# An inference step of a hybrid encoder on one core: the mLSTM's denominators, four weight blocks of the output projection, and four evictions change their place or engine

## The chip, the cores and the metric

The program runs on one NeuronCore of a Trainium2 chip. A core has five engines that run side by side, each its own instructions in a fixed order: TensorE (in profiles PE; its weight loads are PEld), VectorE (DVE), ScalarE (ACT), GpSimd (POOL) and SyncE (SP), which here only starts transfers. They meet at semaphores: an instruction waits until a counter that other engines raise has reached a number. Data lie in SBUF (128 partitions); TensorE writes its products into PSUM, which has eight banks here. The metric is the device time of one launch in microseconds (us); lower is better.

## The reference, cut to what matters

One step of a trunk of two layers over 1024 prompt tokens and 32 sample tokens, model width 1024, all in fp32. Layer 0 mixes with a gated recurrence (RG-LRU) and sliding-window attention side by side, layer 1 with the mLSTM matrix memory. Behind each mixer stands a SwiGLU and a gated per-layer term.

```python
# layer 0: attention of a chunk's queries over its own and the two earlier chunks, with sinks
s = einsum('...qkgd,...skd->...kgqs', q, k) * B_HEAD_DIM ** -0.5 + bias      # bias = -slope * distance
p = softmax(concatenate([s, sink], axis=-1), axis=-1)[..., :-1]
o = einsum('...kgqs,...skd->...qkgd', p, v)
y = concatenate([y_a, o], axis=-1) @ w_out                                   # y_a from the recurrence

# layer 1: one chunk of the mLSTM
s = einsum('nthd,nshd->nhts', q, k) * dw
num = einsum('nhts,nshd->nthd', s, v) + w_prev * einsum('nthd,nhde->nthe', q, c_m)
den = s.sum(axis=-1) + w_prev * einsum('nthd,nhd->nht', q, n_m)
norm = maximum(abs(den), exp(-m_t))
h = num / norm
c_new = decay * c_m + einsum('nhs,nshd,nshe->nhde', ws, k, v)
n_new = decay * n_m + einsum('nhs,nshd->nhd', ws, k)
```

## The kernel before, in words

Activations lie feature-major, 8 tiles of 128 features by 1056 tokens, in thirds of 352 tokens. Every projection is three fp32r products (L456 to L458): high part of the weights times high part of the input, and the two mixed ones. `x` is split into `xh` and `xl`, a weight block (128 output features by 1024 inputs) into `wh` and `wl`.

The weights come as a stream of 208 blocks through two raw buffers (`raw`, filled by SyncE) and four slots (`wh`, `wl`). For block b, GpSimd's loop (L521 to L542) waits until the block has landed and until TensorE has finished the block that held the slot (`block_done`); then it makes the high part (L540, the raw block plus zero) and the low part (L542, raw minus high), and the low part's end frees the raw buffer (`raw_free`), for which TensorE waits before it reads the slot. For the blocks in the list `ACT_HIGH` ScalarE makes the high part instead (`weight_high`, L1710), and GpSimd waits for it and makes only the low part. Blocks 14 to 17 (B0_OUT and the three behind it) are the first four of layer 0's output projection; ScalarE makes their high parts in the attention's loop (`HIGH_AT`).

**Attention.** Nine query blocks n of 128 tokens (the last has 32), each with two halves h = 2n and 2n + 1 by key head. All four engines run loops over n that are written out by hand and meet by counts. TensorE: transpose the probabilities of h = 2n (`transpose_p`, L684), scores of block n + 2 (`scores`, L668), transpose h = 2n + 1, a fill, the outputs (`outputs`, L702), at times a second fill. A fill is one unit of a projection, 24 matmuls over one third of the tokens, put there to keep TensorE busy: fills 0 to 7 are the query projection, with blocks 10 to 13, and fills 8 to 15 the output projection, with blocks 14 to 17. `FILL_A` and `FILL_B` say which fill stands in which n. Fill f, from the fourth on, waits until fill f - 1 is evicted (`fill_free`), since from there all share bank 7.

VectorE's loop (L1444 on): `shares` (L1383 to L1388) sums and inverts the exponents' sums and, for even h, multiplies the probabilities; `biased` (L1362) adds the distances to the scores, four instructions that read PSUM, and takes the maxima; `maxima` (L1375, L1376) makes of these what ScalarE's exponents need; `filled` evicts a fill (L1427 for fills 0 to 7, L1417 for the others); `y_low` (L1403) and `first_out_low` (L1408) make low parts of the output projection's input, for which fill 8 waits. ScalarE's loop: `copy_p` (L1952, PSUM to `pts`) twice, `divide` (L1942), `weight_high`, `exps` (L1928, L1931), `y_high` (L1968), `out_high` (L1964), `exps`.

**mLSTM.** Nine chunks of 128 tokens (n = 0 is the sample's, then the prompt's in order). TensorE: `front` makes keys and queries (L908), transposes the keys (L917) and multiplies them (L924); `chunk` makes the numerators, the state's part (L943, `across`) and the chunk's own (L950, `within`), and the state's updates (L978), eight products through four banks, so that the fifth waits until VectorE has read the first (`cup_read`), and the next chunk's `front` for nearly all of them. VectorE's `chunk`: numerators (L1618), the rest of the last chunk's norm (L1602), the denominators (L1632, L1633, L1635, three small instructions that wait for each other), the updates (`update`, L1597), the last chunk's low part (L1579), the division (L1645), the next chunk's weighted product `sw` (`weigh`, L1571, for which TensorE's L950 waits), the norm's statistics (L1656). GpSimd adds the causal mask to the next chunk's decays (`mask`, L516), and makes the first blocks of layer 1's output projection behind the first two masks.

Of the kernel before, what the change touches and what calls it, by code (L numbers as in the profile page):

```python
# [46 lines left out]
B0_OUT = B0_IN + B_IN0  # L47
B0_FFN = B0_OUT + B_OUT0
B0_PLE = B0_FFN + B_FFN
B1_GATE = B0_PLE + B_PLE  # L50
# [4 lines left out]
B1_FFN = B1_OUT + 8  # L55
# [35 lines left out]
def build(nc, I, O):  # L91
    with ExitStack() as ctx:
# [121 lines left out]
        high_made = sem("high_made")  # L214


        ACT_HIGH = [1, 2, 3] + [B0_OUT + j for j in range(4)] + [b for b0 in (B0_FFN, B1_GATE, B1_FFN) for b in (b0, b0 + 1)]
        zero_ready = sem("zero_ready")
        block_done = sem("block_done")
        acc_done = sem("acc_done")  # L220
# [168 lines left out]

        FILL_A = {0: 4, 1: 6, 2: 7, 4: 9, 5: 11, 6: 12, 7: 14}  # L390
        FILL_B = {0: 5, 3: 8, 4: 10, 6: 13, 8: 15}

        HIGH_AT = {1: (B0_OUT, B0_OUT + 1), 2: (B0_OUT + 2,), 3: (B0_OUT + 3,)}

        FILL_BANK = (7, 6, 5, 4) + 12 * (7,)

# [604 lines left out]
        def _(dve):  # L1001
# [447 lines left out]
            for n in range(NQ):  # L1449
                if n + 1 < NQ:  # L1450
                    shares(2 * n + 2)
                if n + 2 < NQ:
                    biased(2 * n + 4)
                    maxima(2 * n + 4)
                if n + 1 < NQ:
                    shares(2 * n + 3)
                filled(FILL_A.get(n))
                if n + 2 < NQ:
                    biased(2 * n + 5)
                    maxima(2 * n + 5)  # L1460
                if n < NT:
                    y_low(n)
                if n == 3:
                    first_out_low()
                if n in LOW_O and n < NQ - 1:
                    out_low(n)
                filled(FILL_B.get(n))
# [142 lines left out]
            def chunk(n, last, nxt):  # L1610
# [16 lines left out]
                if last is not None:  # L1627
                    for h in range(1, H):
                        normalise(h)
                numerator(3)  # L1630
                dve.wait_ge(num_read, 1 + 4 * n + 4)
                step(dve.scalar_tensor_tensor(st[:, 32:36], iq[:, :, HC], -1.0, iq[:, :, HC], ALU.mult, ALU.max))  # L1632
                step(dve.tensor_tensor(st[:, 32:36], st[:, 32:36],  # L1633
                                       cols[:, ds(TAKEN[n], 1), 2, :].rearrange("p a h -> p (a h)"), ALU.max))
                step(dve.reciprocal(st[:, 36:40], st[:, 32:36]))  # L1635
                for u in range(4):
                    update(n, u)
                for u in range(4, 8):
                    update(n, u)
                if nxt is not None and last is not None:  # L1640
                    out_low(last)
                dve.wait_ge(o_in, 16 * (n + 1))
# [39 lines left out]
        def _(act):  # L1682
# [290 lines left out]
            for n in range(NQ):  # L1973
                copy_p(2 * n)
                copy_p(2 * n + 1)
                if n == 0:
                    exps(2)
                    exps(3)
                if n == 3:
                    act.wait_ge(mix_low, LOW_Y[2])  # L1980
                    act.dma_start(x[:, 0:4, :], I["xT"][:, 0:4, :]).then_inc(x_in, 16)
                    act.wait_ge(oh_ready, 3)
                    act.activation(xh[:, 4:8, 0:3 * P], qt0[:, :, 0:3 * P], ACT.Copy).then_inc(yh_ready, 1)
                if n == NQ - 1:
                    act.wait_ge(s_done, 2 * NQ)
                    act.wait_ge(mix_low, LOW_O012)
                    act.dma_start(x[:, 4:8, :], I["xT"][:, 4:8, :]).then_inc(x_in, 16)
                if n + 1 < NQ:
                    divide(2 * n + 3)
                for b in HIGH_AT.get(n, ()):  # L1990
                    weight_high(b)
                if n + 2 < NQ:
                    exps(2 * n + 4)
                if n < NT:
                    act.wait_ge(y_ready, AT)
                    if n > 0:

                        act.wait_ge(fill_free, 4 * n)
                    y_high(n)
                if n < NQ - 1:  # L2000
                    out_high(n)
                if n + 2 < NQ:
                    exps(2 * n + 5)
# [338 lines left out]
```

## Time and profile before

| | us |
|---|---|
| median of 3 runs | 2697.84 (2696.9 to 2699.97) |
| profiled execution | 2697.7 |
| its span in the trace | 2695.9 |
| TensorE busy | 2640.4 (98%) |
| VectorE busy | 1433.8 (53%) |
| GpSimd busy | 933.4 (35%) |
| ScalarE busy | 622.9 (23%) |

The span is the time from the first to the last instruction that the profiler recorded. Busy is the time in which an engine ran an instruction. The clock granted to TensorE is full throughout. The attention's loop lies between 189 and 300 us of the span, the mLSTM's chunks between 1563 and 1705 us. In a row of a timeline the first number is the start in us from the span's start, the second how long the instruction (or the group, with its count behind x) took, and the bracket at its end how long the engine had been idle before it and who ended that.

### The profile page before, as it was taken

The page shows a single profiled execution, that of the slowest core. Times are in us where ns is not written, and L with a number is a line of the kernel's source. Part 1 is how long each engine was busy: PE and PEld are TensorE (multiplying, and loading weights), DVE is VectorE, ACT ScalarE, POOL GpSimd, SP SyncE. Part 2 cuts the span into 40 slices and gives each one's busy share as a digit, 9 for nine tenths or more (in the row PEclk, how much of TensorE's full clock was granted, in tenths as well). Part 3 has the DMA queues.
Part 4 walks back from the last instruction along what each step waited for, and adds up shares of the span by engine and source line. Part 5 has one row for each costly group of instructions (what it writes and reads, how often), then busy time and mean ns, then how long its engine had stood idle before and what let it go on. Part 6 is the DMA issues. An engine that isn't in the chain of part 4 may idle for free.

```text
span 2695.9 us, 40972 instructions
## 1 busy us (share of the span) xinstructions
PE 2640.4 (98%) x17188; PEld 2579.6 (96%) x17188; DVE 1433.8 (53%) x2358; ACT 622.9 (23%) x1316; POOL 933.4 (35%) x435
## 2 busy tenths in 40 slices
PE   8998999999999999999999999999999999999997
PEld 7886899999999999999999977999999999999997
DVE  7966555444444444667773058654444444444566
ACT  4548331000000000224132157331000000000043
POOL 3311234333333344333433310224443433333430
PEclk9999999999999999999999999999999999999999
DMA  4101211111111111113133232311111111111111
GB/s 146 50 17 64 80 47 48 48 40 47 43 44 47 48 48 47 48 48 129 47 90 102 95 102 90 136 40 48 47 48 47 40 48 40 47 48 48 55 40 65
DMA packets 65488, 162.49 MB, mean 60 GB/s; under 512 B 7696, under 2 KB 36368, under 8 KB 64408
## 3 DMA queue, kind: packets, MB, share of 16 engines
q1 hardware_dynamic: 35312, 115.17, 13.7%
q10 hardware_dynamic: 29992, 44.70, 4.9%
q8 instruction: 136, 2.23, 0.3%
q14 instruction: 48, 0.39, 0.0%
HBM read 139.43 MB, written 20.42 MB: 59 GB/s over the span
## 4 chain that ended last, share of the span: by engine, by line
PE 91%; DVE 4%; ACT 3%; issue 1%; ACTq 0%; DVEq 0%
PE ps L456 29%; PE ps L458 29%; PE ps L457 29%; PE ps L978 1%; DVE uc L1299 1%; PE ps L684 0%; ACT ss L1931 0%; PE ps L702 0%; PE ps L908 0%; PE ps L668 0%; ACT ck L2115 0%; DVE lr L1322 0%; PE ps L563 0%; ACT L2143 0%; ACT L2165 0%
## 5 line engine op out<-in xcount | busy, mean ns | idle before, releaser
L456 PE MATMUL ps<-xh,wh 128*128 128x352 f32 x3432 | 1117.0, 325 | 19.2 <-DVE xl L1014 12.2
L457 PE MATMUL ps<-xl,wh 128*128 128x352 f32 x3432 | 1110.3, 324 | 0.0
L458 PE MATMUL ps<-xh,wl 128*128 128x352 f32 x3432 | 1110.3, 324 | 0.0
L540 POOL TENSOR_TENSOR wh<-raw,seeds 128x1024 fp32r<-128x1024 f32 x195 | 398.8, 2045 | 1377.7 <-PE ps L458 1343.5
L456 PEld LDWEIGHTS ps<-xh,wh 128*128 128x128 f32 x3432 | 648.2, 189 | 27.0 <-issue 19.1
L457 PEld LDWEIGHTS ps<-xl,wh 128*128 128x128 f32 x3432 | 648.3, 189 | 1.7
L458 PEld LDWEIGHTS ps<-xh,wl 128*128 128x128 f32 x3432 | 648.2, 189 | 0.0
L542 POOL TENSOR_TENSOR wl<-raw,wh 128x1024 fp32r<-128x1024 f32 x208 | 525.1, 2525 | 206.3 <-ACT wh L1714 127.8
L1129 DVE TENSOR_TENSOR tmpa<-ps,rstd 128x352 f32<-128x352 f32 x132 | 69.1, 524 | 720.1 <-PE ps L458 711.2
L456 PE MATMUL ps<-hh,wh 128*128 128x352 f32 x1056 | 340.4, 322 | 0.0
L458 PE MATMUL ps<-hh,wl 128*128 128x352 f32 x1056 | 340.0, 322 | 0.0
L457 PE MATMUL ps<-hl,wh 128*128 128x352 f32 x1056 | 340.0, 322 | 0.0
L1797 ACT ACTIVATE tmpa<-tmpa 128x352 f32<-128x352 f32 x132 | 66.0, 500 | 1108.1 <-DVE tmpa L1129 1108.0
L1156 DVE TENSOR_TENSOR x<-ps,x 128x352 f32<-128x352 f32 x528 | 259.3, 517 | 110.1 <-PE ps L458 109.8
L458 PEld LDWEIGHTS ps<-hh,wl 128*128 128x128 f32 x1056 | 198.6, 188 | 0.0
L457 PEld LDWEIGHTS ps<-hl,wh 128*128 128x128 f32 x1056 | 198.5, 188 | 0.0
L456 PEld LDWEIGHTS ps<-hh,wh 128*128 128x128 f32 x1056 | 198.4, 188 | 0.0
L1114 DVE TENSOR_TENSOR hl<-tmpb,hh 128x352 fp32r<-128x352 f32 x132 | 179.0, 1357 | 0.0
L456 PE MATMUL ps<-wh,xh 128*128 128x256 f32 x576 | 163.7, 284 | 0.0
L458 PE MATMUL ps<-wh,xl 128*128 128x256 f32 x576 | 162.2, 282 | 0.0
L457 PE MATMUL ps<-wl,xh 128*128 128x256 f32 x576 | 162.2, 282 | 0.0
L1108 DVE TENSOR_TENSOR tmpb<-tmpb,tmpa 128x352 f32<-128x352 f32 x132 | 138.8, 1051 | 0.0
(267 smaller groups left out, 2325.9 us busy)
## 6 DMA issues: line engine op xcount, KB each, us to landing
raw<-wstream SPq DMA_DIRECT2D x208, 512.0 KB, 3.6
vod<-stage ACTq DMA_DIRECT2D x72, 128.0 KB, 1.9
vb<-vod ACTq DMA_DIRECT2D x9, 512.0 KB, 4.0
ob<-vod ACTq DMA_DIRECT2D x9, 512.0 KB, 3.8
x<-xT ACTq DMA_DIRECT2D x2, 2112.0 KB, 8.2
xsave<-x ACTq DMA_DIRECT2D x1, 4224.0 KB, 13.1
x<-xsave ACTq DMA_DIRECT2D x1, 4224.0 KB, 13.4
yT<-ybuf SPq DMA_DIRECT2D x6, 704.0 KB, 3.3
```

The costliest lines, as they stand in the source:

```text
L456: pe.matmul(out, whi, mhi, start=first, stop=False)
L457: pe.matmul(out, whi, mlo, start=False, stop=False)
L458: return pe.matmul(out, wlo, mhi, start=False, stop=last)
L540: pool.tensor_tensor(hi, raw[:, r, :], zero, ALU.add).then_inc(hi_made, 1)
L542: pool.tensor_tensor(lo, raw[:, r, :], hi.bitcast(F32), ALU.subtract).then_inc(raw_free, 1)
L978: pe.matmul(bank((2, 3, 0, 1)[u % 4], HC + 1), kw[:, u, :], vb[:, u // 2, :], start=True, stop=True).then_inc(cup_done, 1)
L1108: dve.tensor_tensor(tmpb[:, v % 3, :], tmpb[:, v % 3, :], tmpa[:, v % 3, :], ALU.mult).then_inc(h32_ready, 1)
L1114: dve.tensor_tensor(hl[:, par, f, tt * TW:(tt + 1) * TW], tmpb[:, v % 3, :], hh[:, par, f, tt * TW:(tt + 1) * TW].bitcast(F32), ALU.subtra ...
L1129: dve.tensor_tensor(tmpa[:, v % 3, :], bank(2 * tt), rstd[:, sl], ALU.mult).then_inc(gate_scaled, 1)
L1156: dve.tensor_tensor(xs, bank(u % 8), xs, ALU.add).then_inc(down_added, 1)
L1299: ins = dve.scalar_tensor_tensor(cv[:, :], ua[:, t, j:j + CA], vec("a_w", 4 * j + t), cv[:, :], ALU.mult, ALU.add)
L1797: act.activation(tmpa[:, v % 3, :], tmpa[:, v % 3, :], ACT.Silu).then_inc(sil_ready, 1)
```

## The change

Three edits. Blocks 14 to 17 leave `ACT_HIGH`, so GpSimd makes both of their parts, and ScalarE's calls in the attention go. In VectorE's attention loop, where n has no second fill (n = 1, 2, 5, 7), the eviction of the first one (fills 6, 7, 11, 14) moves behind the distances and maxima of h = 2n + 5. In VectorE's mLSTM chunk, the eight updates of the state move ahead of the three instructions of the denominators.

```diff
-        ACT_HIGH = [1, 2, 3] + [B0_OUT + j for j in range(4)] + [b for b0 in (B0_FFN, B1_GATE, B1_FFN) for b in (b0, b0 + 1)]
+        ACT_HIGH = [1, 2, 3] + [b for b0 in (B0_FFN, B1_GATE, B1_FFN) for b in (b0, b0 + 1)]
...
-        HIGH_AT = {1: (B0_OUT, B0_OUT + 1), 2: (B0_OUT + 2,), 3: (B0_OUT + 3,)}
...
-                filled(FILL_A.get(n))
+                if n in FILL_B:
+                    filled(FILL_A.get(n))
                 if n + 2 < NQ:
                     biased(2 * n + 5)
                     maxima(2 * n + 5)
+                if n not in FILL_B:
+                    filled(FILL_A.get(n))
...
                 numerator(3)
+                for u in range(8):
+                    update(n, u)
                 dve.wait_ge(num_read, 1 + 4 * n + 4)
                 step(dve.scalar_tensor_tensor(st[:, 32:36], iq[:, :, HC], -1.0, iq[:, :, HC], ALU.mult, ALU.max))
                 step(dve.tensor_tensor(st[:, 32:36], st[:, 32:36],
                                        cols[:, ds(TAKEN[n], 1), 2, :].rearrange("p a h -> p (a h)"), ALU.max))
                 step(dve.reciprocal(st[:, 36:40], st[:, 32:36]))
-                for u in range(4):
-                    update(n, u)
-                for u in range(4, 8):
-                    update(n, u)
...
-                for b in HIGH_AT.get(n, ()):
-                    weight_high(b)
```

The edits shift the line numbers: an instruction's line in the changed kernel is up to four off its line before.

On ScalarE, query block 1 of the attention: before, from the two copies of the probabilities (`pts`) on,

```order
L1952 ACTIVATE pts<-ps 128x1024 x2
L1942 ACTIVATE ss_100<-ss_100,sm 128x256 x4
L1714 ACTIVATE wh<-raw 128x1024 x2
L1928 ACTIVATE sm<-sm 128x4
L1931 ACTIVATE ss_101,sm<-ss_101,sm 128x256 x4
L1968 ACTIVATE xh<-ga 128x4x352
```

and now:

```order
L1952 ACTIVATE pts<-ps 128x1024 x2
L1942 ACTIVATE ss_100<-ss_100,sm 128x256 x4
L1928 ACTIVATE sm<-sm 128x4
L1931 ACTIVATE ss_101,sm<-ss_101,sm 128x256 x4
L1968 ACTIVATE xh<-ga 128x4x352
```

The two high parts (L1714, blocks 14 and 15) are gone, as are those of blocks 16 and 17 further on.

On VectorE, the same query block: before, from the inverse of the sums (L1385) on, the eviction of fill 6 (L1427), the distances of h = 7 (the instruction that writes `ss_100`, four of them), and behind them:

```order
L1385 RECIPROCAL sm<-sm 128x4
L1427 SCALAR_TENSOR_TENSOR qt_106<-ps,qscale,rstd 128x352
L1362 ISA ss_100,sm<-dist,ps 128x256
L1362 ISA sm 128x1
...
L1375 SCALAR_TENSOR_TENSOR sm<-sm,nsink 128x4
L1376 TENSOR_TENSOR sm<-vecs,sm 128x4
L1403 TENSOR_TENSOR xl<-ga,xh 128x4x352
```

and now:

```order
L1383 RECIPROCAL sm<-sm 128x4
L1360 ISA ss_100,sm<-dist,ps 128x256
L1360 ISA sm 128x1
...
L1373 SCALAR_TENSOR_TENSOR sm<-sm,nsink 128x4
L1374 TENSOR_TENSOR sm<-vecs,sm 128x4
L1425 SCALAR_TENSOR_TENSOR qt_106<-ps,qscale,rstd 128x352
L1401 TENSOR_TENSOR xl<-ga,xh 128x4x352
```

The eviction, L1427 before and L1425 now, has moved behind the distances and the maxima.

On VectorE, an mLSTM chunk: before, from the last numerator (`iq`) on, the denominators (`st`), the eight updates (`cs`) and the last chunk's low part,

```order
L1618 TENSOR_TENSOR iq<-ps,iq 128x257
L1632 SCALAR_TENSOR_TENSOR st<-iq 128x4
L1633 TENSOR_TENSOR st<-st,cols 128x4
L1635 RECIPROCAL st<-st 128x4
L1597 SCALAR_TENSOR_TENSOR cs<-cs,decay,ps 128x257 x8
L1579 SCALAR_TENSOR_TENSOR xl<-ps,vecs,xh 128x128 x8
```

and now:

```order
L1620 TENSOR_TENSOR iq<-ps,iq 128x257
L1599 SCALAR_TENSOR_TENSOR cs<-cs,decay,ps 128x257 x8
L1636 SCALAR_TENSOR_TENSOR st<-iq 128x4
L1637 TENSOR_TENSOR st<-st,cols 128x4
L1639 RECIPROCAL st<-st 128x4
L1581 SCALAR_TENSOR_TENSOR xl<-ps,vecs,xh 128x128 x8
```

The updates stand directly behind the numerator, the denominators behind them.

## Rows read from the trace of the kernel before

**Rows 1.** The page's part 1, TensorE and its weight loads: busy us, share.

```profile
PE 2640.4 (98%) x17188; PEld 2579.6 (96%) x17188; DVE 1433.8 (53%) x2358; ACT 622.9 (23%) x1316; POOL 933.4 (35%) x435
```

**Rows 2.** Waits of TensorE, 170 to 330 us: who <- for whom: us, times, longest.

```profile
PE ps L684 <- ACT pts L1952: 8.4, 5, 3.3
```

**Rows 3.** Waits of TensorE, 1560 to 1720 us, same columns.

```profile
PE ps L978 <- DVE cs L1597: 4.0, 7, 2.0
```

**Rows 4.** Timeline of GpSimd, attention: start, us, what [idle before <- releaser].

```profile
214.50 4.70 POOL L542 TENSOR_TENSOR wl<-raw,wh 128x1024 fp32r<-128x1024 f32 x2 [55.17 <-PE ps L458]
```

**Rows 5.** Timeline of VectorE beside GpSimd, attention.

```profile
216.94 2.29 DVE L1376 TENSOR_TENSOR sm<-vecs,sm 128x4 f32<-128x4 f32 x1
...
228.30 0.42 DVE L1362 CUSTOM_DVE_ANT_0 ss<-dist,ps 128x256 f32<-128x256 f32 x1
```

**Rows 6.** Timeline of VectorE, attention, the instructions in question.

```profile
197.41 1.22 DVE L1388 TENSOR_TENSOR ss<-ss,sm 128x1024 f32<-128x1024 f32 x1
...
200.31 0.16 DVE L1376 TENSOR_TENSOR sm<-vecs,sm 128x4 f32<-128x4 f32 x1
...
200.67 0.56 DVE L1427 SCALAR_TENSOR_TENSOR qt<-ps,qscale,rstd 128x352 f32<-128x352 f32 x1
...
205.87 1.62 DVE L1403 TENSOR_TENSOR xl<-ga,xh 128x1408 fp32r<-128x1408 f32 x1 [2.81 <-ACT xh L1968]
...
211.47 0.18 DVE L1385 RECIPROCAL sm<-sm 128x4 f32<-128x4 f32 x1
...
214.40 0.58 DVE L1427 SCALAR_TENSOR_TENSOR qt<-ps,qscale,rstd 128x352 f32<-128x352 f32 x1 [2.76 <-PE ps L458]
...
230.51 1.62 DVE L1403 TENSOR_TENSOR xl<-ga,xh 128x1408 fp32r<-128x1408 f32 x1 [0.60 <-ACT xh L1968]
...
237.60 1.76 DVE L1408 TENSOR_TENSOR xl<-qt,xh 128x1536 fp32r<-128x1536 f32 x1
```

**Rows 7.** Timeline of TensorE, attention.

```profile
197.66 1.94 PE L702 MATMUL ps<-pts,vtok 128*64 128x512 f32 x8
...
201.28 0.43 PE L456 MATMUL ps<-xh,wh 128*128 128x352 f32 x1 [1.68 <-DVE qt L1427]
...
205.26 1.03 PE L684 MATMUL ps<-ident,ss 128*128 128x128 f32 x8
...
222.48 1.06 PE L684 MATMUL ps<-ident,ss 128*128 128x128 f32 x8 [3.30 <-ACT pts L1952]
...
234.07 1.06 PE L684 MATMUL ps<-ident,ss 128*128 128x128 f32 x8 [1.83 <-ACT pts L1952]
...
239.46 0.40 PE L456 MATMUL ps<-xh,wh 128*128 128x352 f32 x1 [1.27 <-issue]
```

**Rows 8.** Timeline of ScalarE, attention.

```profile
211.68 1.71 ACT L1942 ACTIVATE ss<-ss,sm 128x256 f32<-128x256 f32 x4
...
213.29 1.99 ACT L1714 ACTIVATE wh<-raw 128x1024 fp32r<-128x1024 f32 x2
```

**Rows 9.** Timeline of all engines, mLSTM chunks 0 and 1.

```profile
1576.81 3.23 DVE L1597 SCALAR_TENSOR_TENSOR cs<-cs,decay,ps 128x257 f32<-128x257 f32 x8
...
1577.35 2.00 PE L978 MATMUL ps<-vb,kw 128*128 128x257 f32 x8 [2.04 <-DVE cs L1597]
...
1578.94 1.90 POOL L540 TENSOR_TENSOR wh<-raw,seeds 128x1024 fp32r<-128x1024 f32 x1
...
1579.95 4.45 DVE L1645 SCALAR_TENSOR_TENSOR hb<-iq,st,ob 128x256 f32<-128x256 f32 x4
...
1584.66 0.69 DVE L1571 TENSOR_TENSOR sw<-ps,dw 128x512 f32<-128x512 f32 x1 [0.26 <-PE ps L924]
```

**Rows 10.** Timeline of all engines, mLSTM chunk 3.

```profile
1611.81 1.67 DVE L1645 SCALAR_TENSOR_TENSOR hb<-iq,st,ob 128x256 f32<-128x256 f32 x4
...
1615.09 0.69 DVE L1571 TENSOR_TENSOR sw<-ps,dw 128x512 f32<-128x512 f32 x1 [1.62 <-ACT dw L2123]
...
1623.06 2.00 PE L978 MATMUL ps<-vb,kw 128*128 128x257 f32 x8 [0.34 <-DVE cs L1597]
```


## The prediction

> **What bounds the kernel now.** I read the page's first part first: TensorE is busy for 2640.4 us, 98% of the span [rows 1]. So only a stretch in which TensorE waits can give time, and anything that makes it wait longer costs time one for one, since behind each stretch it runs without a gap again. The waits of TensorE in the two stretches that the change touches come next. In the attention it waits 8.4 us in five pieces for ScalarE's copies `pts`, in the program's L684 transposes [rows 2]. In the mLSTM chunks it waits 4.0 us in seven pieces for VectorE's updates `cs` [rows 3]. Last I read the timelines there, engine by engine, and one thing in them decides the forecast: what happens to VectorE while GpSimd runs.
>
> **What a running GpSimd instruction does to VectorE.** L1376 is a sum over 128x4 elements, whose sources both lie in SBUF. It takes 0.16 us alone, as at 200.31 [rows 6]. At 216.94 it took 2.29 us and ended at 219.23, when GpSimd's two low parts (214.50 to 219.20) ended [rows 4, 5]. L1645, four of them, took 4.45 us beside two GpSimd instructions [rows 9]. L1362, which reads one source from PSUM, took 0.42 us in the middle of a GpSimd instruction [rows 5], and so did eight L1597 in 3.23 us [rows 9]. So: a VectorE instruction with two sources in SBUF stands still until the GpSimd instruction ends, one with a source in PSUM does not. The rows agree with the Trainium skill's page "SBUF — State Buffer", section "Who interferes with whom", which states an exclusive lock of a shared port pair that the instruction which issues first keeps to its end.
>
> **Part 1: GpSimd makes both parts of blocks 14 to 17.** It removes four ScalarE copies, 0.95 us each (1.99 for two that overlap by 0.1) [rows 8], and adds four GpSimd instructions of 1.90 us [rows 9] in front of four low parts of 2.35 us [rows 4]. GpSimd had been idle for 55 us before the first low part [rows 4], because that waited for ScalarE's place in its order. Now each pair starts as soon as its slot is free, at the end of fills 4, 5, 6 and 7, in the midst of VectorE's softmax work. I follow it step by step; times are those of the profiled run, shifted.
>
> Fill 4 ends at 197.75 (TensorE's next row is at 197.66, its matmuls overlap) [rows 7]. VectorE's multiplication L1388 holds until 198.63 [rows 6]. GpSimd then works 198.6 to 200.5 (high) and 200.6 to 203.0 (low). L1375 gets in between the two; L1376 needs its result, asks 0.1 us too late and ends at 203.05 instead of 200.47. Behind it in VectorE's order stand L1385, for which ScalarE's division waits, and the eviction L1427 (200.67), for which fill 5 waits. Both come 2.7 us later: fill 5 starts at 203.95, not 201.28, and fill 5 ends at 208.0, not 205.3 [rows 6, 7]. ScalarE is busy from that division to its next copy `pts`, so this is 2.7 us late too.
>
> The second pair runs from 208.2 to 210.1 and onwards. L1403, now asked for at 208.5, waits till 210.1 and runs 1.6; the low part follows, 211.7 to 214.0; L1383 behind it waits for that. Before, L1403 and an eviction had taken it to 207.95, so VectorE is now 6.1 us late. Of the 2.76 us of idle time in front of L1427 at 214.40 [rows 6] nothing helps here, since ScalarE waits for instructions ahead of it. The third pair starts at the end of fill 6, 214.3 + 2.7 = 217.1. L1376 of the next scores stood 0.28 ahead of L1385 at 211.47, and is asked for at 217.3, L1375 0.2 before it. One waits for the high part (to 219.1), and L1383, L1385 behind it for the low part (to 221.6). So L1385 (before at 211.47) is done at 221.85, and ScalarE's division starts at 221.9 and not at 211.68: 10.2 late. From it to the copy that releases L684 at 222.48, ScalarE spends 1.9 less (two copies gone) and 0.25 less (no wait for L1376): +8.0 at that L684. The next one, 234.07, has one more copy of 0.95 gone: +7.05 [rows 7, 8].
>
> Fill 7 came behind the L684 of 222.48, which takes 0.8, and a fill takes 4.0 to 4.1 (201.28 to 205.26) [rows 7]: it ended at 227.4. The fourth pair starts 8.0 later, at 235.4, and runs from 235.5 to 239.85. L1403 (230.51 + 7.05 = 237.56) waits 2.3 us for its low part, or goes first and L1383 behind it waits as long. VectorE has no gap from there to L1408 [rows 6], so L1408 comes at 237.60 + 7.05 + 2.3 = 246.95, and fill 8, which needs it, 9.3 us later than 239.46 [rows 7]. Behind it the remaining waits stay as they were. Part 1 with part 2: **+9.3 us**, of which the fourth copy of ScalarE takes nothing back, since fill 8 waits for VectorE.
>
> **Part 2: VectorE adds the distances (L1362) ahead of the evictions of fills 6, 7, 11 and 14.** The eviction reads PSUM and takes 0.58; the additions no longer wait for the fill, so the scores' exponents are ready earlier. Before, this wait showed on ScalarE as under 0.2 us; the next fill needs the bank a full step later, so the later eviction has cover. Alone it is worth 0 to 0.4 us; it is counted above (the 0.25).
>
> **Part 3: the denominators (L1632, L1633, L1635) behind the eight updates L1597.** In chunks 2 to 7 the update that frees the first bank now comes when the numerator is there. The waits of TensorE for it, 4.0 in all less the first of 2.04, are 1.96 in six pieces, 0.34 in one of them [rows 3, 9, 10]. All of it goes: the updates read PSUM, so GpSimd's mask beside them does not matter. What is late next: the denominators, 0.5 us, now stand before VectorE's L1579 and L1645. Before the next product L1571 VectorE has 1.62 us of idle time [rows 10], so they are covered. **-2.0 us.**
>
> In chunk 0 the wait of 2.04 goes as well: the updates start at 1574.2 and end at 1577.7. But then L1632 meets GpSimd's low part (which ends as the row at 1578.94 starts), L1633 the high part (to 1581.0) and L1645 the second low part, 2.4 us, to 1583.4. Four L1645 of 0.4 end at 1585.0, and L1571 follows at 1585.1, while it stood at 1584.66 [rows 9]. TensorE, 2.0 us early at first, waits for just this product: **+0.45** instead of -2.04. The bounds are these two; I take the upper, since each of the three waits is a row's GpSimd instruction that nothing here moves.
>
> **Sum.** 9.3 - 2.0 + 0.45 = +7.8 us, on the profiled execution's own 2697.7 (1.8 above its span, 0.1 below the median of the runs): 2705.5 us. An effect within 0.2% (5.4 us, 2692.4 to 2703.2) is about what a measurement of this kernel can't tell from no change.
>
> **The rivals.**
> - *VectorE wins the tie at 219.1.* L1383 asks at the very time at which GpSimd asks for its third low part (each some 0.08 us behind the end of the high part). If it gets in, L1385 is done near 219.6 and 2.2 us of the loss go: 2703.3. For it: L1383 needs nothing of L1376, and can follow it without a gap. Against it: between 1578.9 and 1583.3 four L1645 without a gap stood ready, and GpSimd's low part still got in after one of them (their 4.45 us hold 1.67 us of work [rows 9, 10]). Chance 0.22. The rule of the page named above gives the tie to the instruction that issues first; read so, it would be VectorE's, and the sum would be this rival's.
> - *The waits are partly absorbed.* GpSimd starts late enough that one pair falls into VectorE's idle time (2.76 us before 214.40, 3 us before 227.4), or chunk 0 does give its 2.04. Each is worth 2.5; two of them give 2700.5. Chance 0.13.
> - *The other side: the relief of ScalarE decides.* ScalarE's copies lie on the way to L684 twice (1.9 and 0.95), and part 2 adds 0.25: 3.1. If VectorE's small instructions slip in between the GpSimd ones, so that neither the eviction nor L1385 is held up, that is gained, and then chunk 0 gives its 2.04 too: 2697.7 - 3.1 - 4.0 = 2690.6. The point from which it decides is where the added delay of L1385 in the third step falls under the 2.15 us that ScalarE saves there. For it: ScalarE is what TensorE waits for five times [rows 2]. Against it: every meeting of this kind in [rows 5, 9] stood still. Chance 0.09.
> - The forecast keeps 0.56.
>
> **Range and chances.** Worst case: one more low part in the way, +2.4, 2707.9. The range from 2699.5 to 2708.0 holds the forecast and the first two rivals and leaves out the last. Slower by over 0.2%: the forecast and half of the first rival, which lies on that bound, 0.56 + 0.10 = 0.66; within 0.2%: its other half and the second, 0.12 + 0.13 = 0.25; faster 0.09.
>
> **What would show it.** On the profile after: fill 5's first matmul 2.7 us later behind its wait for `qt` (1.7 becomes 4.4); L684's longest wait for `pts` 5 us and not 3.3; the wait in front of fill 8 near 3.5 and not 1.27; VectorE rows of 2 us and more for 128x4 elements at 200 to 222 us; GpSimd's pairs directly at the ends of fills 4 to 7. In the mLSTM the waits of L978 for `cs` gone, and one wait of L950 for `sw` of 3 us or more in chunk 1. The forecast is wrong if the first of these small instructions is not stopped: then fill 5 starts at 201.3, and all that follows from it falls.

## The result and the profile after

The changed kernel takes 2704.32 us in the median (2701.78 to 2706.86, 16 runs), against 2697.81 us before (16 runs). The ratio is 1.0025, with an interval of 1.0018 to 1.0032: slower by 4.9 to 8.6 us. The profiled execution after has a span of 2701.6 us, 5.7 more than before, and a mean granted clock of TensorE of 0.993 (0.997 before). Its single waits can be laid beside those of before. The kernel before was timed again beside each round of experiments (medians 2698.27 to 2698.30 us); every ratio below is to the one of its own round.

The waits of TensorE come first. First those in the attention, 170 to 330 us, then those in the mLSTM, 1560 to 1730 us: what was waited for, us in total, how many, the longest.

```profile
PE ps L682 <- ACT pts L1952: 7.1, 4, 4.2
PE ps L454 <- DVE qt L1425: 4.0, 1, 4.0
PE ps L454 <- issue: 1.8, 1, 1.8
```

```profile
PE ps L948 <- DVE sw L1573: 3.8, 1, 3.8
```

L682 is the L684 of [rows 2]; its waits sum to less than before. The wait for the eviction `qt` of fill 4 has grown from 1.7 to 4.0. In the mLSTM the waits for `cs` of [rows 3] are gone, and the one for `sw` in chunk 1 is 3.8, not 1.0. All waits of TensorE that the profile lists in these two stretches sum to 24.9 us, 25.2 before, though the kernel takes 5.7 us more. What the waits don't hold is seen in the rows of TensorE itself, in the attention:

```profile
198.22 1.94 PE L700 MATMUL ps<-pts,vtok 128*64 128x512 f32 x8
...
204.12 0.66 PE L454 MATMUL ps<-xh,wh 128*128 128x352 f32 x1 [3.96 <-DVE qt L1425]
...
209.52 1.04 PE L682 MATMUL ps<-ident,ss 128*128 128x128 f32 x8
...
226.38 1.94 PE L682 MATMUL ps<-ident,ss 128*128 128x128 f32 x8 [4.18 <-ACT pts L1952]
...
241.42 3.62 PE L700 MATMUL ps<-pts,vtok 128*64 128x512 f32 x8 [1.11 <-ACT pts L1952]
246.80 0.40 PE L454 MATMUL ps<-xh,wh 128*128 128x352 f32 x1 [1.76 <-issue]
```

Against [rows 7], fill 5 starts 2.84 us later (204.12, not 201.28; 0.56 of it was lost ahead of the attention, which starts at 190.40 and not 189.84, and so with every start below), and then takes 5.40 us to the next transpositions, not 3.98. Its first matmul takes 0.66, not 0.43. Eight transpositions take 1.94 at 226.38, not 1.06, and eight outputs L700 3.62 at 241.42, not 1.94. That is near half speed: the lower of the clock's two levels, 1.2 GHz and not 2.4. The windows say the same. Their columns are the stretch, its length, TensorE's busy time, its instructions, the granted clock, the DMA share and GB/s. After:

```profile
204.00:210.00 6.00, 5.88 (x29) 0.73 0.31 91
226.00:234.00 8.00, 7.62 (x36) 0.68 0.01 2
1580.00:1600.00 20.00, 15.35 (x125) 0.83 0.58 171
```

In the same three stretches before, the granted clock is 1.00 throughout. A clock of 0.73 is a mean over both levels: fill 5's first ten matmuls start 0.29 us apart and those behind them 0.16. But the clock of before is not full in the whole program, though the part on the time before says so. From 280 to 300 us it is 0.91, and a fill at the attention's end runs its first matmuls at the low level:

```profile
293.71 0.66 PE L456 MATMUL ps<-xh,wh 128*128 128x352 f32 x1
```

GpSimd's pairs in the attention, high part and low part:

```profile
198.43 2.51 POOL L538 TENSOR_TENSOR wh<-raw,seeds 128x1024 fp32r<-128x1024 f32 x1 [38.54 <-PE ps L456]
201.02 2.34 POOL L540 TENSOR_TENSOR wl<-raw,wh 128x1024 fp32r<-128x1024 f32 x1
209.83 2.24 POOL L538 TENSOR_TENSOR wh<-raw,seeds 128x1024 fp32r<-128x1024 f32 x1 [6.47 <-PE ps L456]
212.15 2.38 POOL L540 TENSOR_TENSOR wl<-raw,wh 128x1024 fp32r<-128x1024 f32 x1
217.53 1.89 POOL L538 TENSOR_TENSOR wh<-raw,seeds 128x1024 fp32r<-128x1024 f32 x1 [3.00 <-PE ps L456]
219.50 2.36 POOL L540 TENSOR_TENSOR wl<-raw,wh 128x1024 fp32r<-128x1024 f32 x1
233.70 1.89 POOL L538 TENSOR_TENSOR wh<-raw,seeds 128x1024 fp32r<-128x1024 f32 x1 [11.83 <-PE ps L456]
235.67 2.36 POOL L540 TENSOR_TENSOR wl<-raw,wh 128x1024 fp32r<-128x1024 f32 x1
```

and VectorE beside them, each row with start and duration:

```profile
201.00 0.16 DVE L1374 TENSOR_TENSOR sm<-vecs,sm 128x4 f32<-128x4 f32 x1
201.08 2.31 DVE L1381 TENSOR_TENSOR sm<-sm 128x4 f32<-128x4 f32 x1
...
210.73 1.36 DVE L1381 TENSOR_TENSOR sm<-sm 128x4 f32<-128x4 f32 x1
...
212.34 3.27 DVE L1386 TENSOR_TENSOR ss<-ss,sm 128x1024 f32<-128x1024 f32 x1
...
217.36 0.15 DVE L1381 TENSOR_TENSOR sm<-sm 128x4 f32<-128x4 f32 x1
...
235.68 3.84 DVE L1401 TENSOR_TENSOR xl<-ga,xh 128x1408 fp32r<-128x1408 f32 x1 [1.50 <-ACT xh L1968]
```

The first pair makes a row of 2.31 us of L1381 (four numbers per partition, 0.16 alone). The second makes one of 1.36 of it and stops the multiplication L1386 for 2 (3.27, where it takes 1.22 at 197.97). The fourth stops L1401 for 2.2 (3.84, not 1.62). The third pair stops nothing that counts: the instructions it should have met were through at 217.5, as it began. L1381 had started 0.17 us before it.

In the mLSTM, VectorE behind the updates of chunk 0:

```profile
1580.51 3.47 DVE L1599 SCALAR_TENSOR_TENSOR cs<-cs,decay,ps 128x257 f32<-128x257 f32 x8
1583.89 1.94 DVE L1636 SCALAR_TENSOR_TENSOR st<-iq 128x4 f32<-128x4 f32 x1
1585.86 1.81 DVE L1637 TENSOR_TENSOR st<-st,cols 128x4 f32<-128x4 f32 x1
...
1587.92 3.63 DVE L1645 SCALAR_TENSOR_TENSOR hb<-iq,st,ob 128x256 f32<-128x256 f32 x4
1591.59 0.69 DVE L1573 TENSOR_TENSOR sw<-ps,dw 128x512 f32<-128x512 f32 x1
```

and TensorE, which waits for that `sw` and then runs at the low level:

```profile
1583.38 1.98 PE L906 MATMUL ps<-uu,cbd 64*64 64x128 f32 x64
...
1592.42 1.39 PE L948 MATMUL ps<-vb,sw 128*128 128x257 f32 x4 [3.82 <-DVE sw L1573]
1594.37 2.08 PE L948 MATMUL ps<-vb,sw 128*128 128x257 f32 x4 [0.55 <-DVE iq L1617]
...
1597.96 1.91 PE L930 MATMUL ps<-ident,hb 128*128 128x128 f32 x8
```

For the sum I cut TensorE's timeline at three kinds of mark: "A" runs from the attention's first group of transpositions (189.84 before) to its last (291.54), "B" from the first matmul of chunk 0 of the mLSTM to that of chunk 2, "C" from there to that of chunk 8. All kernels below are measured by these; times in us.

| stretch | before | after | difference |
|---|---|---|---|
| up to A | 189.84 | 190.40 | +0.56 |
| A, attention | 101.70 | 108.45 | +6.75 |
| between A and B | 1271.52 | 1270.62 | -0.90 |
| B, chunks 0 and 1 | 30.26 | 33.03 | +2.77 |
| C, chunks 2 to 7 | 95.46 | 91.73 | -3.73 |
| behind C | 1007.12 | 1007.37 | +0.25 |

The six differences add up to the +5.7 of the spans.

### The profile page after: what moved, and what is told of

It reads as the page before. It is cut to its first block and busy times, and to the rows that moved or that the text cites. A ratio compares the mean times of both kernels' runs of the same rounds, so it can differ in the third digit from the quotient of the medians.

```text
span 2701.6 us, 40967 instructions
## 1 busy us (share of the span) xinstructions
PE 2646.0 (98%) x17188; PEld 2585.9 (96%) x17188; DVE 1437.0 (53%) x2358; ACT 618.7 (23%) x1312; POOL 940.0 (35%) x439
## 5 line engine op out<-in xcount | busy, mean ns | idle before, releaser
L538 POOL TENSOR_TENSOR wh<-raw,seeds 128x1024 fp32r<-128x1024 f32 x199 | 404.9, 2035 | 1449.8 <-PE ps L456 1413.8
```

The costliest lines, as they stand in the source:

```text
L538: pool.tensor_tensor(hi, raw[:, r, :], zero, ALU.add).then_inc(hi_made, 1)
```

## The experiments

The theory: a GpSimd instruction that reads SBUF holds up VectorE's next instruction with two sources in SBUF until it ends, and the length of that one instruction is the price. The rivals: GpSimd's work or bandwidth in total; the new order of instructions by itself; TensorE's lower clock as the real cause.

**The parts alone.** Each was built into the kernel before; the whole diff stands above, so only what each holds is told. Part 1 (both parts of blocks 14 to 17 by GpSimd):

> The kernel before with part 1 alone: GpSimd makes both parts of blocks 14 to 17, the rest as before. Theory (GpSimd's reads stop VectorE's instructions with two sources in SBUF): the whole loss of the change sits here, the attention ends 5 to 8 us later, and the time is 2703 to 2706, ratio 1.002 to 1.003; the wait in front of fill 5 is 4 us as in the profile after, and not 1.7. Rival (the loss comes from the mLSTM's order or from the new order of evictions): within 1 us of before.

Measured: 2705.69 us, ratio 1.0026 (1.0015 to 1.0036). A is 110.06, B 30.28, C 94.61. The wait before fill 5 is 3.97, that of the whole change. A is 8.4 longer, a little more than the 5 to 8 expected. Here, with the eviction of fill 6 in its old place, the third pair did hit: the first of the two rows of `maxima`, at 220.08, took 2.34 us.

Part 3 (denominators behind the updates):

> The kernel before with part 3 alone: the eight updates ahead of the denominators. From the two profiles: chunks 0 and 1 together 2.8 us longer, chunks 2 to 7 together 3.7 us shorter, so 2697 against 2697.8, a ratio between 0.999 and 1.000, and a wait of TensorE for the product sw of 3 to 4 us in chunk 1. Rival (the shift in chunks 0 and 1 comes from the late attention and not from the order): 3.7 to 6 us faster, a ratio of 0.998 and no such wait.

Measured: 2695.37 us, ratio 0.9991 (0.9982 to 1.0000). A 103.57, B 32.69, C 91.74, so the loss in chunks 0 and 1 and the gain in 2 to 7 are both part 3's. Fill 5 waits 1.7 as before. The time is 1.6 us under the 2697 expected.

Parts 2 and 3:

> The changed kernel without part 1: ScalarE makes the high parts again, the evictions and the updates stay moved. Theory: the loss goes, 2696 to 2697.5, ratio 0.9995 or so, and fill 5 waits 1.7 us as before. Rival (part 2 costs by itself, since a fill's bank comes free later): above 2698.5.

Measured: 2697.42 us, ratio 0.9995 (0.9986 to 1.0004). A 102.26, B 32.83, C 91.72.

Part 2 (the distances ahead of four evictions):

> Part 2 alone: VectorE adds the distances ahead of the evictions of fills 6, 7, 11 and 14. Theory: the score exponents start earlier, but every fill behind them has cover, so 0 to 0.4 us less, 2697.4 to 2698.3, ratio 0.9998 to 1.0000. Rival (the evictions come later and with them a fill or a transposition; parts 2 and 3 together stood 2 us above part 3 alone, which may be this or the scatter of the runs): 1 to 2 us more, 1.0004 to 1.0008.

Measured: 2699.09 us, ratio 1.0001 (0.9993 to 1.0010). A 102.26, B 30.50. Neither side is shown: the interval holds both. A is 0.56 above before, and its window from 210 to 226 us has a granted clock of 0.90, which part 3 alone (0.89), without this order, has too. So part 1 carries the loss in the attention, part 3 the loss and the gain in the mLSTM. What part 2 is worth stays open: parts 2 and 3 stood 2.05 us above part 3 alone, part 2 alone 0.8 above before, each just within the scatter, so a cost of up to 2 us is not ruled out, and beside part 1 it may save something (A 108.45 with it, 110.06 without).

**Is it TensorE's clock?** In the changed kernel three groups of matmuls were issued twice, with the same results, so that TensorE has less idle time ahead of the waits:

```diff
-                for g in range(4):
+                rounds = 2 if n == 4 else 1
+                for g in [g for _ in range(rounds - 1) for g in range(4)] + [4, 5, 6, 7]:
+                    last, g = g >= 4, g % 4
...
-                for kk in range(2):
+                for kk in (0, 1, 0, 1) if n == 0 else (0, 1):
...
-                for h in range(H):
+                for h in (0, 1, 2, 3, 0, 1, 2, 3) if n == 1 else range(H):
```

> The changed kernel with three groups of matmuls done twice, each just ahead of a long wait of TensorE and with the same result: the outputs of query block 0, the scores of query block 4, and the product of keys and queries of mLSTM chunk 1, some 1.9 us of work each, inside waits of about 4 us. In the profile of the changed kernel the granted clock is 0.84 to 0.88 behind these waits and fill 5 takes 5.4 us, not 4.0. Theory (TensorE's wait itself brings the lower clock, and that is a second cost beside the wait): with less idle time the clock stays, fill 5 takes 4.0 again, the transposes and fill 7 take 4.9 and not 7.1, chunk 1 2.3 less; 2699 to 2701, a ratio below 1.0015. Rival (the slow matmuls come from something else, or the extra work delays those who wait for it): 2704 or more.

Measured: 2702.95 us, ratio 1.0014 (1.0005 to 1.0022), 1.4 us under the changed kernel by the medians, which is within the runs' scatter, and above the 2699 to 2701 of the theory. A 107.81, B 31.16.

```profile
198.23 3.65 PE L702 MATMUL ps<-pts,vtok 128*64 128x512 f32 x16
204.14 0.43 PE L454 MATMUL ps<-xh,wh 128*128 128x352 f32 x1 [2.26 <-DVE qt L1427]
...
226.41 1.06 PE L684 MATMUL ps<-ident,ss 128*128 128x128 f32 x8 [2.35 <-ACT pts L1954]
...
239.23 1.94 PE L702 MATMUL ps<-pts,vtok 128*64 128x512 f32 x8 [1.11 <-ACT pts L1954]
244.61 0.40 PE L454 MATMUL ps<-xh,wh 128*128 128x352 f32 x1 [3.45 <-issue]
...
250.11 1.04 PE L684 MATMUL ps<-ident,ss 128*128 128x128 f32 x8
```

The transpositions at 226.41 and the outputs at 239.23 are back at full speed (1.06 and 1.94), and fill 8 starts 2.19 us earlier, at 244.61. VectorE is earlier by as much: its eviction of fill 7 starts at 231.39 and not at 233.59, because that fill ran at full clock, and with the eviction everything up to L1408, for which fill 8 waits. So the low clock behind the wait of 4.18 cost A 2.2 us. But here fill 8 falls to the low level in its turn: it takes 5.50 us to the transpositions at 250.11, where it takes 3.96 in the changed kernel. That gives 1.54 back, and A is only 0.64 shorter. Fill 5 stayed slow (granted clock 0.72 from 204 to 210 us) though its wait was 2.26. In chunk 1 nothing covers the clock: B falls by 1.87 of its excess of 2.77, at a clock of 0.91 from 1580 to 1600 us, not 0.83. The span is only 0.4 shorter, since between A and B this profile is 2.4 us longer, with a clock of 0.96 from 298 to 340 us.

So the clock is a second cost beside the waits, in the attention as in the mLSTM. The edit moved the low stretches more than it removed them, and no run here shows the changed kernel at full clock. The lateness of VectorE is there all the same, and it is no effect of the clock: fill 5 starts at 204.14 here.

**The length of one GpSimd instruction.** The changed kernel with the same elements of blocks 14 to 17 in more and shorter instructions:

```diff
+                parts = 4 if b in (B0_OUT, B0_OUT + 1, B0_OUT + 2, B0_OUT + 3) else 1
+                w_ = KT * P // parts
+                zero_ = seeds[:, 6:7].to_broadcast([P, w_])
...
-                    pool.tensor_tensor(hi, raw[:, r, :], zero, ALU.add).then_inc(hi_made, 1)
+                    for q in range(parts):
+                        ins = pool.tensor_tensor(hi[:, q * w_:(q + 1) * w_], raw[:, r, q * w_:(q + 1) * w_], zero_, ALU.add)
+                    ins.then_inc(hi_made, 1)
...
-                pool.tensor_tensor(lo, raw[:, r, :], hi.bitcast(F32), ALU.subtract).then_inc(raw_free, 1)
+                for q in range(parts):
+                    ins = pool.tensor_tensor(lo[:, q * w_:(q + 1) * w_], raw[:, r, q * w_:(q + 1) * w_],
+                                             hi[:, q * w_:(q + 1) * w_].bitcast(F32), ALU.subtract)
+                ins.then_inc(raw_free, 1)
```

> The changed kernel, with GpSimd's high and low part of blocks 14 to 17 each made by four instructions of a quarter of the size (128 x 256 instead of 128 x 1024): the same elements, only the length of one instruction is cut. Theory (a GpSimd instruction that reads SBUF holds up VectorE's next instruction with two SBUF sources until it ends): such a stop is at most some 0.6 us (a quarter of 2.4) instead of up to 2.4, so fill 5 waits some 2.0 to 2.8 us instead of 3.96, the attention's T0 to T17 comes back from 108.5 to 103.5 to 105.5 us, and the time is 3 to 5 us under the changed kernel's: 2699 to 2701.5, ratio to before 1.000 to 1.0015. Rival (the two engines share the bandwidth, or GpSimd's total work counts, not the length of one instruction): the same 1.0025, T0 to T17 at 108. Chunks 0 and 1 of the mLSTM are as in the changed kernel by both (33 us), since blocks there are not cut.

Measured: 2697.83 us, ratio 0.9998 (0.9989 to 1.0007). The halves, with `parts = 2`:

> The changed kernel with GpSimd's high and low part of blocks 14 to 17 each in two instructions of half the size (128 x 512). Theory (one GpSimd instruction is what VectorE waits out, and the loss goes with its length): a stop is at most some 1.2 us; fill 5 waits 2.3 to 3.2 us (3.96 whole, 2.05 in quarters), T0 to T17 is 103.5 to 106.5 us, between 108.5 whole and 102.4 in quarters, and the time lies between too, 2699 to 2702. Rival (below some length the stop no longer matters, or quarters win by another effect such as the moment at which GpSimd starts): as the quarters (2698, 102.4) or as the whole (2704.3, 108.5).

Measured: 2701.18 us, ratio 1.0007 (0.9999 to 1.0016). Both came out as the theory had it, the quarters in A and in time somewhat better than forecast. GpSimd in quarters:

```profile
198.24 2.94 POOL L542 TENSOR_TENSOR wh<-raw,seeds 128x256 fp32r<-128x256 f32 x4 [38.31 <-PE ps L456]
201.26 2.82 POOL L546 TENSOR_TENSOR wl<-raw,wh 128x256 fp32r<-128x256 f32 x4
206.31 4.69 POOL L542 TENSOR_TENSOR wh<-raw,seeds 128x256 fp32r<-128x256 f32 x4 [2.23 <-PE ps L456]
...
215.24 2.32 POOL L542 TENSOR_TENSOR wh<-raw,seeds 128x256 fp32r<-128x256 f32 x4 [1.32 <-PE ps L456]
```

and VectorE beside it:

```profile
200.67 0.53 DVE L1382 TENSOR_TENSOR sm<-vecs,sm 128x4 f32<-128x4 f32 x1
201.12 0.15 DVE L1389 TENSOR_TENSOR sm<-sm 128x4 f32<-128x4 f32 x1
```

Four quarters take 2.32 us alone, more than one whole (1.89), so GpSimd does more in all. Yet the rows of the small sums, stop included, are now at most 0.68 us long, as the 0.53 here. The price is shared: between the quarters VectorE gets in, and GpSimd waits in its turn (4.69 at 206.31, beside L1409's 1.81). The series:

| blocks 14 to 17 in | wait before fill 5 | A | time | ratio |
|---|---|---|---|---|
| one instruction | 3.96 | 108.45 | 2704.32 | 1.0025 |
| two halves | 3.04 | 105.02 | 2701.18 | 1.0007 |
| four quarters | 2.05 | 102.40 | 2697.83 | 0.9998 |
| (before: ScalarE makes the high parts) | 1.68 | 101.70 | 2697.81 | 1 |

The loss follows the length of one instruction, with the same work on the same engine. That excludes bandwidth and total work. (The ratios are to the kernel before in the same round, 2698.3 us for the halves and the quarters.) The wait before fill 5 is the cleanest of the columns. A and the time hold TensorE's low stretches too, which the quarters don't escape either:

```profile
222.18 1.94 PE L690 MATMUL ps<-ident,ss 128*128 128x128 f32 x8 [2.27 <-ACT pts L1960]
```

B went from 33.03 to 31.28 as well, although its blocks were not cut and 33 was expected. Its wait for `sw` is still 3.8, but the granted clock from 1580 to 1600 us is 0.91, not 0.83. Nothing of the edit reaches there, so I take this for scatter of the clock; with one profile of each it is not shown.

**Chunk 0 of the mLSTM, three ways.** All three start from parts 2 and 3 (2697.42 us, B 32.83). The first keeps the old order in chunk 0 alone:

```diff
+                if n == 0:
+                    denominators()
                 for u in range(8):
                     update(n, u)
...
+                if n > 0:
+                    denominators()
```

> Parts 2 and 3 of the change without part 1, and the denominators ahead of the updates in chunk 0 as before, behind them in chunks 1 to 7. Theory (in chunk 0 alone GpSimd's two blocks stand beside the denominators, and moved behind the updates these are stopped longer and carry chunk 1's sw with them): chunks 0 and 1 take 30.3 us as before instead of 32.8, chunks 2 to 7 keep 91.7, no wait for sw over 1.5 us; 2.5 us less than parts 2 and 3: 2694.5 to 2695.5, ratio 0.9985 to 0.999. Rival (the 2.4 us of chunk 1 come from the new order itself, or from TensorE's state there): chunks 0 and 1 stay over 32 us, ratio 0.9995.

Measured: 2695.74 us, ratio 0.9990 (0.9982 to 0.9999); B 30.32, C 91.73. The wait of 2.1 for `cs` in chunk 0 is back, and that for `sw`, 3.4 in parts 2 and 3, is 1.0 as before. So the 2.5 us in chunks 0 and 1 come from the order in chunk 0 alone, as expected; the median is a little above the forecast, 1.7 us under parts 2 and 3.

The second keeps GpSimd's blocks away from the first chunks:

```diff
                 if b == B1_OUT + 2:
-                    mask(0)
-                    mask(1)
-                if b == B1_OUT + NW:
-                    for n in range(2, CH):
+                    for n in range(CH):
                         mask(n)
+                    pool.wait_ge(num_read, 1 + 4 * CH)
```

> Parts 2 and 3 of the change without part 1; GpSimd makes all the chunks' masks first and the blocks from 2 blocks into out1 on only after chunk 7's numerators are read, so that it reads nothing of size while VectorE makes chunk 0's denominators. Theory (GpSimd's reads stop VectorE's small instructions): the rows of the denominators in chunk 0 are 0.2 us each instead of 1.5 and 1.8, chunks 0 and 1 take 27.9 to 28.9 us instead of 32.8, chunks 2 to 7 keep 91.7, and if the stage behind has its blocks in time, the time is 4 to 5 us under parts 2 and 3: 2692.5 to 2694, ratio 0.998. Rival: the blocks made late stop VectorE in the last chunk or make the next stage's first matmuls wait, and give back 1 to 4 us behind chunk 7 (then chunks 0 and 1 are still under 29 us). Rival 2: chunks 0 and 1 stay over 32 us, then it isn't GpSimd.

Measured: 2692.10 us, ratio 0.9978 (0.9969 to 0.9987); B 27.92, C 91.73. VectorE behind the same updates:

```profile
1577.47 0.16 DVE L1635 SCALAR_TENSOR_TENSOR st<-iq 128x4 f32<-128x4 f32 x1
1577.66 0.16 DVE L1636 TENSOR_TENSOR st<-st,cols 128x4 f32<-128x4 f32 x1
...
1578.08 1.67 DVE L1644 SCALAR_TENSOR_TENSOR hb<-iq,st,ob 128x256 f32<-128x256 f32 x4
1582.32 0.69 DVE L1572 TENSOR_TENSOR sw<-ps,dw 128x512 f32<-128x512 f32 x1 [2.56 <-PE ps L922]
```

What took 7.7 us in the changed kernel from L1636 to L1645's end (7.2 in parts 2 and 3) takes 2.3, and VectorE now waits 2.56 us for TensorE, not the reverse. The blocks made later kept nobody waiting, so neither rival held.

The third cuts the two blocks beside chunk 0 in quarters and leaves them where they are (`parts = 4 if b in (B1_OUT + 2, B1_OUT + 3) else 1`):

> Parts 2 and 3 without part 1, with GpSimd's high and low parts of the two blocks that stand beside chunk 0 each in four instructions of a quarter of the size. The same elements at the same place. Theory (the length of one GpSimd instruction is what counts): the denominators' first two rows together take at most 1.3 us instead of 3.3, chunks 0 and 1 take 29 to 31 us instead of 32.8, 2694 to 2696 in all, ratio 0.9985 to 0.999. Rival (the total of GpSimd's work counts): 32.8 us and 0.9995, as parts 2 and 3 uncut.

Measured: 2692.57 us, ratio 0.9979 (0.9970 to 0.9988); B 28.07, C 91.76.

```profile
1578.34 0.55 DVE L1645 SCALAR_TENSOR_TENSOR st<-iq 128x4 f32<-128x4 f32 x1
1578.92 0.65 DVE L1646 TENSOR_TENSOR st<-st,cols 128x4 f32<-128x4 f32 x1
...
1579.82 3.07 DVE L1654 SCALAR_TENSOR_TENSOR hb<-iq,st,ob 128x256 f32<-128x256 f32 x4
```

B and the time are better than I expected (28.1, not 29 to 31; 2692.6, not 2694 to 2696): with `sw` in time, there is neither the wait nor the low clock behind it (1.00 from 1580 to 1600 us).

**Quarters everywhere.** Without part 1:

> Parts 2 and 3 without part 1, with every one of GpSimd's 403 halves of weight blocks in four instructions of a quarter of the size, not only the two blocks beside chunk 0. GpSimd's busy time grows from 924 to some 1100 us, which its idle time covers. Theory: in the other stages TensorE seldom waits for VectorE, so only the pieces of its waits for VectorE there that are stops by GpSimd go; 0 to 3 us under the kernel with two blocks cut: 2690 to 2693. Rival: the longer GpSimd work is late for the fills somewhere (waits for wl or wh appear) or its reads slow VectorE more than before: 2693 to 2698.

Measured: 2694.84 us, ratio 0.9984 (0.9975 to 0.9993), 2.3 us over the kernel with two blocks cut, so the rival held. A begins 2.8 us earlier than with two blocks cut (187.26, not 190.10), but then TensorE waits for GpSimd. Its waits from 296 to 340 us, which the kernel with two blocks cut has none of:

```profile
PE ps L456 <- POOL wl L548: 2.5, 2, 1.6
```

With part 1 (the whole change):

> The whole change, with every half of a weight block that GpSimd makes in four instructions of a quarter of the size. Against the same without part 1 it tells what part 1 itself is worth once its stops are short. Theory (part 1's cost was the length of the stops alone; four ScalarE copies fewer are worth up to 1 us): T0 to T17 at 101.5 to 103 us, time within 1 us of the kernel without part 1 in quarters, 2691 to 2693.5. Rival (GpSimd's work beside the softmax costs VectorE whatever its pieces): 1.5 to 3 us more than without part 1.

Measured: 2695.31 us, ratio 0.9986 (0.9977 to 0.9994), with A 102.59 and B 27.93. The two differ by 0.5 us, less than their runs scatter (2692 to 2696.5 each), and both are above the 2691 to 2693.5 expected of this one. So part 1 is worth nothing that can be measured, either way, once its stops are short. That is the sum of the copies taken off ScalarE and of the short stops that are left; the test does not part the two.

## Why the prediction was right

The forecast was 2705.5, the measured median 2704.3. The mechanism, VectorE stopped by GpSimd, was there and cost time at three of the four pairs in the attention and in chunk 0 of the mLSTM. That the number came so near was in good part luck: the stops cost about half of what was forecast, and TensorE's low clock, which the prediction did not have, made up for it. It cost 2.2 us of A (fill 8's start with the outputs and scores doubled, 244.61 and not 246.80) and 2.25 of B (below). Without these two the profile would be some 1.3 us above before and not 5.7: an estimate from the rows of single profiles, by which the change would be too small to tell from none.

- **What a running GpSimd instruction does to VectorE.** Right, and tested: stops of 2.31, 1.94 and 1.81 us for instructions on four numbers per partition, gone with the GpSimd instruction (0.16 and 0.16 in the kernel with late blocks) and shrunk with its length. The rule of the Trainium skill's page "SBUF — State Buffer", section "Who interferes with whom", that an instruction with two sources in SBUF contends with a GpSimd instruction that reads SBUF, held in every meeting shown here, and in both directions.
- **Fill 5.** Forecast to start at 203.95 behind a wait of 4.4; it started at 204.12 behind 3.96. Of the 2.84 us, 0.56 came from ahead of the attention; the wait itself grew by 2.28, where 2.7 was forecast. It was L1381 that was stopped and not L1374 (the prediction's L1376). L1374 came in between the pair (201.00, GpSimd's next row 201.02), and L1381, 0.08 later, did not.
- **The third pair: failed.** The step said that L1376 (now L1374) and L1383 behind it would meet the high and the low part, and make the next L684 8.0 us late. It was 3.9 us late (226.38, against 222.48). The sums went through at 217.1 to 217.5, just ahead of GpSimd's 217.53, so the inverse L1383 came at 217.54 and not at 221.85. The second pair too hit others than forecast: L1401 got ahead of it, and L1381 and L1386 were stopped. The fourth stopped L1401 for 2.2, as forecast. In all **A grew by 6.75, where 9.3 was forecast**, and 2.2 of it is the clock, which I had not foreseen: what is left, the stops less ScalarE's relief, is some 4.6, half of the forecast. Two of the signs failed: the longest wait for `pts` is 4.2 and not 5, and the one in front of fill 8 is 1.76 and not near 3.5, because the outputs ahead of it ran at the low level (3.45 where they did not).
- **Chunks 0 and 1: mis-sized.** +0.45 was forecast, +2.77 came. VectorE did as the prediction worked it out: from the start of chunk 0 to the start of `sw` it was 21.60 us before and is 22.12 now, +0.52. The missing 2.3 is TensorE at its low level after the wait of 3.82: from the start of `sw` to the first matmul of chunk 2 it is 10.91 us (1591.59 to 1602.50), 8.66 before, and 8.65 (1582.32 to 1590.97) in the kernel with late blocks, which has the new order and a clock of 1.00. Without the low clock B would be near 30.8.
- **Chunks 2 to 7: mis-sized.** -2.0 was forecast from the idle time in front of L978, -3.73 came. From the start of the transpositions L932 to the next chunk's first matmul it is 4.09 before (1605.00 to 1609.09) and 3.60 after (1614.18 to 1617.78), where the row's idle time is 0.20. The stop cost more than the row shows as idle, 0.49 for 0.20 in this chunk and 0.62 for a whole chunk on average. The idle time of a row counts from the modelled end of the matmuls before it, which overlap; the distance from start to start is the measure.
- **The relief of ScalarE: right for the first two copies.** L1383, for which ScalarE's division waits, came 6.07 us late (217.54, not 211.47), and L682 behind it only 3.90: 2.17 were taken back, where 2.15 was forecast. With quarters the inverse came 1.87 late (213.34) and the transpositions at 222.18 0.30 early. The third copy's 0.95 can't be seen: fill 7 at the low clock ends later, and ScalarE waits 1.23 us for its eviction. The relief is real, but the stops that come with it cost as much or more.
- **The rivals.** The tie at 219.1 never came up, since VectorE was ahead of the third pair altogether. Half of the second rival came true, as the third pair fell beside VectorE's reads of PSUM and its idle time (2.69 us before 222.83); its other half did not. The relief did not decide.

By terms: -2.55 for A, +2.32 for B, -1.73 for C, and -0.09 for what lies around them. They take the forecast of +7.8 to the profile's +5.7. The medians say +6.5.

What stays open is when TensorE's clock falls. It did so behind waits of 3.8 to 4.2 us. Behind the 3.30 of before (222.48) it did not, but behind 3.36 at the same place in part 3 alone, whose attention is the code of before, it did (1.94 for the eight transpositions), and so it did behind 2.27 with quarters (222.18). The wait of 3.8 for `sw` cost B 33.03 in one kernel and 31.28 in another. Part 3 alone has a clock of 0.89 from 210 to 226 us and 0.80 from 226 to 234, and A is 103.57 and not 101.70. With only one profile of each kernel, differences in A of some 1.9 us are not told apart from this; and C differs by 0.85 between before and part 1 alone (95.46 and 94.61), whose mLSTM is the same.

## What to carry to other kernels

An instruction moved to GpSimd can cost its own length on VectorE's path: look which VectorE instructions with two SBUF sources stand beside it, and what waits behind them. Start it later, or cut it into pieces of some 0.6 us where VectorE is on the path, and leave it whole where TensorE waits for GpSimd; the best kernel here, parts 2 and 3 with GpSimd's blocks behind chunk 7, takes 2692.1 us, 0.9978 of before, and the one with only the two blocks beside chunk 0 in quarters is not told apart from it (2692.6). And read a stall of TensorE from start to start, for its price can include the clock behind it.

## What the runs showed of the hardware

- The two engines' stops are mutual. GpSimd's high part at 198.43 took 2.51, not 1.89, as L1386 held until 199.1; four quarters took 4.69, not 2.32, where VectorE's long instructions got in between.
- The gap of 0.08 us between two GpSimd instructions is enough for a VectorE instruction that is ready (L1374 at 201.00), not for the next one.
- The length of a wait alone did not tell whether TensorE's clock fell. It fell behind waits of 3.82, 3.96 and 4.18 (1.94 for eight transpositions, not 1.06), behind 2.26 (fill 5 with the outputs issued twice, clock 0.72) and 2.27 (222.18 with quarters), and at 241.42 behind two short ones of 0.87 and 1.11 (3.62 for eight outputs, not 1.94). It did not fall behind 3.30 (222.48 before; behind 3.36 there in part 3 alone it did) or 2.05 (fill 5 with quarters). Here a low clock cost up to 2.3 us a time where nothing covered it.
